# Input projection of a hybrid decoder trunk: keys and values and the queries each as two chunks of 512 columns by four row blocks

## The reference

```python
h = rms_norm(x, attn_norm[l])
proj = h @ w_in[l]
(gq, gk, gv, gz, gb, ga, nq, kcmp, vcmp, kslc, vslc, kwin, vwin, ngate,
 cb, cc, cx) = jnp.split(proj, split_at, axis=-1)
```

## Time and profile before

| | us |
|---|---|
| median of 3 runs | 1388.76 |
| profiled execution | 1389.11 |
| its span | 1387.4 |
| TensorE busy (matmul) | 1363.8 |
| VectorE busy | 625.6 |
| GpSimd busy | 617.9 |
| ScalarE busy | 507.6 |
| DMA, mean GB/s over the span | 83 |

### The profile page before, as it was taken

One profiled execution on the slowest core, in us unless ns is written; L12 is line 12 of the kernel. 1 busy time (PEld: TensorE's weight loads), 2 busy tenths in 40 slices (PEclk: granted clock), 3 DMA queues, 4 the chain that ended last, 5 costly groups with the idle time before them and its releaser, 6 DMA issues.

```text
span 1387.4 us, 19860 instructions
## 1 busy us (share of the span) xinstructions
PE 1363.8 (98%) x8298; PEld 1165.4 (84%) x8298; DVE 625.6 (45%) x1022; ACT 507.6 (37%) x872; POOL 617.9 (45%) x333
## 2 busy tenths in 40 slices
PE   7999999999999999999999999999999999999998
PEld 6898987799888888888879999777988888888887
DVE  5638577724334213442165386766234432134421
ACT  5564335624323212222346442456242222123210
POOL 4458317633334444443344663266334334434442
PEclk9999999999999999999999999999999999999999
DMA  7325300124342233333222542010233332333322
GB/s 186 99 69 136 88 7 1 32 62 72 100 109 91 84 95 110 91 91 113 85 85 71 121 116 61 1 32 2 63 91 91 101 105 84 107 105 91 92 84 84
DMA packets 182218, 114.76 MB, mean 83 GB/s; under 512 B 46192, under 2 KB 169328, under 8 KB 182128
## 3 DMA queue, kind: packets, MB, share of 16 engines
q1 hardware_dynamic: 180016, 113.22, 29.1%
q10 hardware_dynamic: 2112, 0.26, 0.1%
HBM read 109.80 MB, written 3.67 MB: 82 GB/s over the span
## 4 chain that ended last, share of the span: by engine, by line
PE 91%; DVE 4%; SPq 2%; issue 1%; ACT 1%; DMA 1%; POOL 0%; DVEq 0%
PE ps L621 73%; PE ps L926 3%; PE ps L731 2%; PE ps L909 2%; PE ps L883 2%; PE ps L985 2%; SPq L329 1%; DVE att L1960 1%; DVE st L272 1%; DMA w_raw<-in_w_in 1%; PE ps L657 1%; PE ps L711 1%; PE ps L844 1%; PE ps L961 0%; PE ps L762 0%
## 5 line engine op out<-in xcount | busy, mean ns | idle before, releaser
L1462 POOL TENSOR_TENSOR w_lo<-w_raw,w_hi 128x2048 fp32r<-128x2048 f32 (+3 forms) x98 | 443.4, 4525 | 614.7 <-ACT w_hi L1129 557.7
L1129 ACT ACTIVATE w_hi<-w_raw 128x2048 fp32r<-128x2048 f32 (+1 forms) x100 | 188.6, 1886 | 561.3 <-PE ps L621 551.0
L621 PE MATMUL ps<-hT_hi,w_lo 128*128 128x512 f32 x928 | 231.1, 390 | 0.0
L621 PE MATMUL ps<-hT_hi,w_hi 128*128 128x512 f32 x896 | 224.5, 392 | 1.8 <-POOL w_lo L1462 1.3
L621 PE MATMUL ps<-hT_lo,w_hi 128*128 128x512 f32 x896 | 222.6, 390 | 0.0
L621 PEld LDWEIGHTS ps<-hT_hi,w_lo 128*128 128x128 f32 x928 | 173.5, 188 | 36.0 <-issue 0.3
L621 PEld LDWEIGHTS ps<-hT_hi,w_hi 128*128 128x128 f32 x896 | 166.5, 188 | 36.9 <-POOL w_lo L1462 1.5
L621 PEld LDWEIGHTS ps<-hT_lo,w_hi 128*128 128x128 f32 x896 | 167.8, 188 | 34.9 <-issue 0.3
L2012 DVE TENSOR_TENSOR aT_lo<-ffn_tmp,aT_hi 128x512 fp32r<-128x512 f32 x44 | 141.9, 3225 | 30.7 <-ACT aT_hi L1139 30.7
L2077 DVE TENSOR_TENSOR ffn_tmp<-ps,ffn_tmp 128x512 f32<-128x512 f32 x44 | 30.4, 692 | 243.8 <-ACT ffn_tmp L1423 243.8
L621 PE MATMUL ps<-w_hi,aT_hi 128*128 128x512 f32 (+1 forms) x544 | 123.1, 353 | 0.0
(11 more groups left out here) (316 smaller groups left out, 1683.0 us busy)
## 6 DMA issues: line engine op xcount, KB each, us to landing
w_raw<-in_w_gate_up SPq DMA_DIRECT2D x88, 512.0 KB, 5.1
w_raw<-in_w_in SPq DMA_DIRECT2D x20, 1024.0 KB, 5.3
w_raw<-in_w_down SPq DMA_DIRECT2D x16, 1024.0 KB, 5.0
w_raw<-in_w_out SPq DMA_DIRECT2D x32, 256.0 KB, 4.3
w_raw<-in_w_down SPq DMA_DIRECT2D x8, 768.0 KB, 4.5
w_raw<-in_w_in SPq DMA_DIRECT2D x2, 1120.0 KB, 5.6
w_raw<-in_w_in SPq DMA_DIRECT2D x2, 1056.0 KB, 7.7
x_tok<-in_x SPq DMA_DIRECT2D x4, 512.0 KB, 5.4
```

What stands on the lines that cost most here:

```text
L621: mm = nc.tensor.matmul(out_ap, a(ab, k), b(bb, k), start=first and i == 0, stop=last and i == len(kts) - 1)
L1129: nc.scalar.activation(whi[:, c % 2, 0:kt * w], raw[:, c % 2, 0:kt * w], ACT.Copy).then_inc(S["w_hi"], 1)
L1462: nc.gpsimd.tensor_tensor(wlo[:, c % 2, 0:kt * w], raw[:, c % 2, 0:kt * w], whi[:, c % 2, 0:kt * w].bitcast(F32), ALU.subtract).then_inc(S ...
```

## The change

- Keys and values (512 columns, the old kvs and the first 256 columns of kvw) become two chunks of 512 columns by 4 row blocks ("A": rows 0 to 511 of `w_in`, "B": rows 512 to 1023), numbers 4 and 5; so do the queries, numbers 8 and 9. The size of a chunk stays 1 MB.
- The work of such a pair is 8 groups of 3 parts; a part is 4 matmuls of 512 columns for one token block t, one half and one pass. `PAIR` writes their order out as (t, half, pass). Token block 0 ends in the fifth group's second part and block 1 in its third; block 2 in the seventh group, block 3 in the eighth. Chunk A is done with the sixth group.
- A token block's result fills one whole bank. Each pair uses four banks in the turn of three, so block 3 takes the bank of block 0 and waits until that is emptied. The last two groups of the loop take banks 1 and 0.
- ScalarE empties a token block in one copy of 512 columns. It splits chunk 6 and chunk 10 behind the sixth group of the pair, the moment A's slot is free.
- The 24 branch gates are loaded by a DMA of their own behind zg's 264 columns, which makes 288; ScalarE copies them out with the output gates.
- For chunks of kind C, and for B, TensorE waits for the high parts at the first pass and for the low parts only at the third.
- On SyncE the DMAs of the diagonal blocks and of w1 stand ahead of chunk 8's load, in a function `diagonal_in`.

```diff
-              ("zg", GZ, 264, "T"), ("kvs", KS, 256, "T"), ("kvw", KWN, 280, "T"),
-              ("cmp", KC, 256, "C"), ("cc", CC, 256, "C"), ("nq0", NQ, 256, "T"), ("nq1", NQ + 256, 256, "T"),
+              ("zg", GZ, ZG + 3 * NH, "T"),
+              ("kv", KS, 512, "A"), ("kv", KS, 512, "B"),
+              ("cmp", KC, 256, "C"), ("cc", CC, 256, "C"),
+              ("nq", NQ, 512, "A"), ("nq", NQ, 512, "B"),
+    PAIR = (((0, 0, 0), (0, 0, 1), (0, 0, 2)), ((1, 0, 0), (1, 0, 1), (1, 0, 2)),
+            ((0, 1, 0), (0, 1, 1), (1, 1, 0)), ((1, 1, 1), (2, 0, 0), (2, 0, 1)),
+            ((2, 0, 2), (0, 1, 2), (1, 1, 2)), ((3, 0, 0), (3, 0, 1), (3, 0, 2)),
+            ((2, 1, 0), (2, 1, 1), (2, 1, 2)), ((3, 1, 0), (3, 1, 1), (3, 1, 2)))
+    PAIR_MM = (0, 0, 0, 0, 2, 1, 1, 1)
+    PAIR_TILES = ((), (), (), (), (0, 1), (), (2,), (3,))
+    BANKS = [b % IN_BANKS for b in range(len(BANK_USERS) - 2)] + [1, 0]
...
+        def diagonal_in(sp, l):
+            sp.wait_ge(*S.at("A", NT, l))
+            for b in range(4):
+                sp.dma_start(d_in[b]...).then_inc(S["d_in"], 16)
+            sp.wait_ge(*S.at("d_in", 64, l))
+            for half in range(2):
+                sp.dma_start(Dm[half * HEAD:(half + 1) * HEAD]...).then_inc(S["Dm"], 16)
+            sp.wait_ge(*S.at("gram", NT, l))
+            for k in range(2):
+                sp.dma_start(w1c[:, k], ...).then_inc(S["w1"], 16)
         def sync_layer(sp, l):
             for c in range(2, N_CHUNKS):
+                if c == 8:
+                    diagonal_in(sp, l)
                 sp.wait_ge(*S.at("w_lo", c - 1, l))
...
+                    if name == "zg":
+                        sp.dma_start(dst[:, :, ZG:w], src[:, :, NGT:NGT + w - ZG]).then_inc(S[f"w_in{c % 2}"], 16)
+                        src, dst = src[:, :, c0:c0 + ZG], dst[:, :, 0:ZG]
+                    else:
+                        k0 = KD // 2 if kind == "B" else 0
+                        src = src[:, k0:k0 + kt, c0:c0 + w]
...
-                if c == 8:
-                    sp.wait_ge(*S.at("A", NT, l))
-...
+                if kind == "A":
+                    pair_part(n, *PAIR[g][part])
+                    return
+                if g == 0 and part == 0:
+                    pe.wait_ge(*S.at("w_hi" if kind == "C" else "w_lo", c + 1, l))
+                if g == 0 and part == 2 and kind == "C":
+                    pe.wait_ge(*S.at("w_lo", c + 1, l))
...
+            def pair_part(n, t, half, part):
+                c = GROUPS[n][0] + half
+                if part == 0 and half == 0:
+                    if t == 0:
+                        pe.wait_ge(*S.at("w_lo", c + 1, l))
+                    bank_free(n, t)
+                if t == 0 and half == 1 and part == 0:
+                    pe.wait_ge(*S.at("w_hi", c + 1, l))
+                if t == 0 and half == 1 and part == 2:
+                    pe.wait_ge(*S.at("w_lo", c + 1, l))
+                W, h = (slot(whi, c, KD // 2, 512), slot(wlo, c, KD // 2, 512)), (hhi, hlo)
+                hp, wp = ((0, 0), (1, 0), (0, 1))[part]
+                for k in range(KD // 2):
+                    mm = nc.tensor.matmul(ps[:, in_bank(n, t), :], h[hp][:, half * KD // 2 + k, t * P:(t + 1) * P], W[wp][:, k, :], ...)
+                if part == 2 and (half == 1 or t == NT - 1):
+                    mm.then_inc(S["mm"], 1)
...
+                used = (c + (1 if last else 0)) if paired(n) else c
-                if last and c + 2 < 13:
-                    split_hi(c + 2)
+                if last and used + 2 <= N_IN:
+                    split_hi(used + 2)
...
+                if paired(n) and g == 5:
+                    split_hi(used + 2)
```

More of the change, by code:

```diff
@@ L109, in trunk, with paired, mm_through, tile_done @@
     N_CHUNKS = FFN0 + 2 * PER_HALF
+    PAIR = (((0, 0, 0), (0, 0, 1), (0, 0, 2)), ((1, 0, 0), (1, 0, 1), (1, 0, 2)),
[3 rows of a table added]
+    PAIR_MM = (0, 0, 0, 0, 2, 1, 1, 1)
+    PAIR_TILES = ((), (), (), (), (0, 1), (), (2,), (3,))
     GROUPS = [(c, g, "dve" if CHUNKS[c][0] in ("gq", "gk", "gv", "cx", "cb") else "act")
-              for c in range(N_IN) for g in range(2 if CHUNKS[c][3] == "C" else NT)]
+              for c in range(N_IN) if CHUNKS[c][3] != "B"
+              for g in range({"C": 2, "T": NT, "A": len(PAIR)}[CHUNKS[c][3]])]
     IN_BANKS = 3
[L115 to L122, removed]
+    def paired(n):
+        return CHUNKS[GROUPS[n][0]][3] == "A"
+    def mm_through(n):
+        return sum(PAIR_MM[GROUPS[m][1]] if paired(m) else 1 for m in range(n + 1))
+    def tile_done(n, t):
+        return mm_through(n) - (1 if t == 0 else 0)
+    def banks_before(n):
+        return sum(len(PAIR_TILES[GROUPS[m][1]]) if paired(m) else 1 for m in range(n))
+    def bank_number(n, t):
+        return banks_before(n - GROUPS[n][1]) + t if paired(n) else banks_before(n)
+    BANK_USERS = [e for n, (_, g, e) in enumerate(GROUPS) for _ in (PAIR_TILES[g] if paired(n) else (0,))]
+    BANKS = [b % IN_BANKS for b in range(len(BANK_USERS) - 2)] + [1, 0]
+    def in_bank(n, t=0):
+        return BANKS[bank_number(n, t)]
+    def last_user(n, t):
+        b = bank_number(n, t)
+        return max((u for u in range(b) if BANKS[u] == BANKS[b]), default=None)
+    def emptied(b):
+        return BANK_USERS[b], BANK_USERS[:b + 1].count(BANK_USERS[b])
     with ExitStack() as ctx:
@@ L238, in chunk_shape @@
             if c < N_IN:
-                return KD, CHUNKS[c][2]
+                return KD // 2 if CHUNKS[c][3] in "AB" else KD, CHUNKS[c][2]
             if c < FFN0:
@@ L402, in loads @@
         def loads(c):
-            return sum(4 if N_IN <= i < FFN0 else 2 if i >= FFN0 and (i - FFN0) % PER_HALF < FT else 1
+            return sum(4 if N_IN <= i < FFN0 else 2 if i >= FFN0 and (i - FFN0) % PER_HALF < FT else 2 if i < N_IN and CHUNKS[i][0] == "zg" else 1
                        for i in range(2 + c % 2, c + 1, 2))
@@ L646, in in_group, with bank_free @@
                                part, range(KD), part == 0, part == 2, done)
+            def bank_free(n, t):
+                b = last_user(n, t)
+                if b is not None:
+                    e, v = emptied(b)
+                    pe.wait_ge(*S.at("ev_" + e, v, l))
+            def pair_part(n, t, half, part):
[11 more added lines that the diff above has]
+                for k in range(KD // 2):
+                    mm = nc.tensor.matmul(ps[:, in_bank(n, t), :], h[hp][:, half * KD // 2 + k, t * P:(t + 1) * P], W[wp][:, k, :],
+                                          start=half == 0 and part == 0 and k == 0, stop=half == 1 and part == 2 and k == KD // 2 - 1,
+                                          skip_group_check=True)
+                if part == 2 and (half == 1 or t == NT - 1):
+                    mm.then_inc(S["mm"], 1)
             def cmp_first():
-                pe.wait_ge(*S.at("ev_act", 14, l))
+                pe.wait_ge(*S.at("ev_act", 10, l))
                 pe.wait_ge(*S.at("w1", 32, l))
@@ L1888, in vector_layer @@
                 if name == "cx":
-                    dve.wait_ge(*S.at("mm", n + 1, l))
-                    dve.wait_ge(*S.at("ev_act", emptied(n - 1)[1] if g == 0 else emptied(n - 2)[1], l))
+                    dve.wait_ge(*S.at("mm", mm_through(n), l))
+                    dve.wait_ge(*S.at("ev_act", 16, l))
                     dve.wait_ge(*S.at("gtr", 6, l))
```

79 lines of the change are left out of this document (39 added, 40 removed).

## The result

| | before | after |
|---|---|---|
| median, us | 1388.85 (1387.42 to 1388.93, 4 runs) | 1399.83 (1396.01 to 1402.57, 4 runs) |
| profiled execution, us | 1389.11 | 1400.7 |
| its span, us | 1387.4 | 1399.0 |
| mean granted TensorE clock | 1.00 | 0.993 |

The change makes the kernel slower: ratio 1.0077 (95% interval 1.0063 to 1.0091). The forecast was 1389.2 with a range up to 1392.4; the time lies 7 us beyond it. The span grew by 11.6 us.

What follows compares the result with a forecast made beforehand. TensorE, busy 98% of the span, was taken to bound the kernel. The new gap's +0.4 and +1.7 less 1.72 behind it gave +0.4 us: 1389.5 for the profiled execution, 1389.2 as median, range 1383.6 to 1392.4.

Steps and rivals of the forecast that it cites:

- TensorE's stream: Input projections: TensorE reaches the compression matmul 2.40 us earlier in layer 0, 1.10 in layer 1, and wins 0.86 behind it.
- the removed gap: TensorE's idle time at 40.98 in layer 0, waiting for GpSimd's low part of the third chunk: 1.30 us saved.
- keys, values and gates together: Groups 10 to 17 save 2.06 us a layer; the 24 gate columns in the output gates' chunk cost 0.96.
- The rule that it set against the gain: Skill's matmul gap, columns over 2.4 GHz plus 2.5 ns: halving the matmuls would be worth 0.5 us a layer, not 2.6.
- Gap 1: TensorE idle ahead of the compression matmul (L657 before), because chunk 8 loads behind w1 and delays ScalarE's split; 2.8 us.
- the term of 15.72 from first store to landing: SyncE: chunk 8's load lands 15.72 us after the first small store, taken from chunk 9's landing behind w1.
- far bound, 17.15: Latest landing of chunk 8 after the first small store, from the 9.6 us the 1056 KB load took.
- Behind it the waits are slack: After the compression matmul: the small diagonal DMAs move earlier, so the solve's results arrive before the first hop needs them.
- the like move of chunk 6: Chunk 6's slot frees two groups later; costed at nothing, as its low part is needed only in the third pass.
- a low part that ends later: SyncE's later w_out loads are issued behind it; costed at nothing, as they are read only after the projection.
- Its own sign of being wrong: Forecast fails if ScalarE starts chunk 8's split on TensorE's end, or TensorE waits elsewhere for over 1 us.
- The granted clock is full throughout: Read from the profile before: TensorE's clock is already full, so nothing was expected from it.

Runs made afterwards that it cites:

- both: Changed kernel with VectorE's second compressed-key normalising moved to group 26 and chunk 8's load put ahead of the w1 loads; 1384.81 us, ratio 0.9976.
- c8_before_w1: Changed kernel with the w1 loads put behind chunk 8's load on SyncE; 1394.97 us, ratio to before 1.0052.
- before_norm: Kernel before the change, with only VectorE's second compressed-key normalising moved one group earlier, to group 26; 1391.34 us, ratio 1.0021.
- old_order_norm: Changed kernel with the second normalising in group 26 and SyncE's old order, diagonal DMAs and w1 behind chunk 8's load; 1390.54 us, ratio 1.0016.
- both_act: Kernel of both, with the solved blocks' loads shared two and two between SyncE and ScalarE instead of three and one; 1389.21 us, ratio 1.0004.
- norm_early: Changed kernel with VectorE's second compressed-key normalising moved to group 26, behind the first; 1390.63 us, ratio to before 1.0017.

## Why the prediction was wrong

- **TensorE's stream: right in kind, a little too good.** 2.22 and 0.76 us up to the compression matmul against 2.40 and 1.10. That layer 0 comes so near is in part luck: the removed gap gave 0.22 more than its price and hides that keys, values and gates together gave 0.81 and not 1.10.
- **The rule that it set against the gain was none.** The Trainium skill's "TensorE: Matmul & The Clock Gate", section "Back-to-back issue gap", gives the formula with 2.5 ns for a single isolated matmul, and says that in a stream of weight loads and matmuls both set the spacing. The 0.2263 and 0.1200 us of this stream say nothing for or against that formula.
- **Gap 1: right in place, cause and, for layer 0, size.** 2.43 against 2.8 us. In layer 1 4.02 against a forecast of 2.8: the term of 15.72 from first store to landing was up to 17.18, because the four small stores landed 1.5 us late, likely for the instruction packet among them. The rows of the kernel before have no such packet there; the forecast's far bound, 17.15, covers it all the same.
- **The failed step: "Behind it the waits are slack".** This sentence looked at the diagonal solve alone. What the runs showed in its place is gap 2. The change also moves ScalarE's split of chunk 10 from group 25 to behind group 27, and with it GpSimd's low part, by 5.9 us (144.88 to 150.75). The prediction costed the like move of chunk 6 at nothing, since TensorE needs the low part only in the third pass, and of chunk 10's it saw only that the loads of w_out stand behind "a low part that ends later". It asked who needs the moved work's *result*. It did not ask what runs *beside* the moved work in its new place. That cost 5.3 us of idle TensorE and 3 to 5 us of clock. Its own sign of being wrong, a wait of TensorE elsewhere for over 1 us, came true at L837.
- **The sentence is wrong for the solve too, by less.** Gap 1 hid it: in `both`, where the gaps are gone, the first hop waits 0.72 and 0.34 us for the solved blocks.
- **The trace of before had the clue.** On VectorE an operation of 128 x 62, two inputs in SBUF, took 2.25 us and ended with GpSimd's low part (129.59 + 4.62 = 134.21); a neighbour of the same shape and kind took 0.22:

```profile
132.04 2.25 DVE L1618 TENSOR_TENSOR arena<-arena 128x62 f32<-128x62 f32 x1
...
134.56 0.22 DVE L1620 TENSOR_TENSOR arena<-arena 128x62 f32<-128x62 f32 x1
```

- The Trainium skill's "SBUF — State Buffer", section "Who interferes with whom", states this rule: VectorE and GpSimd share a pair of ports, taken for a whole instruction, and tensor_scalar in a two-port mode or any operation with two SBUF inputs can wait for it. The runs agree, with 4.42, 1.14 to 1.21 and 2.48 us for operations of 0.16 us. Asked of the moved low part, the rule could have named gap 2.
- **The clock: not in the forecast at all.** "The granted clock is full throughout, so nothing is expected from there" was read from a kernel without long gaps in this part. A gap of 2.64 us cost another 1.6 to 4.5 us (12.64 - 8.16, layer 0 of c8_before_w1), 0.6 to 1.7 times its own length.
- The range was worked out from one unknown, chunk 8's landing. Moved work on GpSimd had no term, so no bound.

## What to carry to other kernels

When an edit moves an instruction, list what stands beside it in the new place on the engine it shares ports with, and look in the old trace for small operations that last many times as long as their twins and end together with a neighbour engine's large one. Such a hold counts as busy time, so no list of waits shows it. When two loads change places in a queue, follow both: of three orders here one held up ScalarE, one VectorE, and the third cost least. If a large edit loses time while its own stream is faster, take away the new waits one at a time and then together; `both` turned 1399.8 into 1384.8, below the 1388.3 to 1388.9 of before.

## What the hardware showed beyond that

- A tiny operation is held as well as a larger one: 62 numbers waited 4.42 us. Cutting GpSimd's operation into four doesn't help a chain of small operations, as each waits again.
- Additions of 128 x 512 that read PSUM and one SBUF tile passed at 0.69 us beside GpSimd's low part (before_norm, 144.16), and so did a reduction of 31 x 128 with its usual 0.27 us (145.39).
- The granted clock fell to 0.50 behind idle times of TensorE of 2.43, 2.64 and 4.02 us, and to 0.56 to 0.59 in windows of 2 us behind 2.71 (old_order_norm, layer 1) and 2.87 (both_act); it stayed at 1.00 behind 0.72, 0.79, 0.93, 1.26 and once behind 2.25 (norm_early, layer 0, to 122). It came back at 165 to 166 in layer 0 and at 855 in layer 1, so the same gap cost 3.4 and 1.7 us by the windows, and 4.5 by the timeline in layer 0 of c8_before_w1.
- Four equal stores from one queue had landed, by the loads that wait for them, 3.37 us after the first issue in one layer and 4.93 in the other. The late ones had one packet of the "instruction" queue among them, in each of six kernels; the issue time (1.95, 3.44, and 1.96 in a late case) doesn't tell.
